# Last expert round: row-block stores on GpSimd's queue, the accumulator read in the mixing, one pair load ahead of the router

## What is computed

```python
probs = softmax(h @ router_w + router_b)
top_p, top_i = top_k(probs, 2)            # two of 8 experts for each position
gates = sum(one_hot(top_i) * top_p / sum(top_p))
for e in range(8):                        # D_FF_EXPERT = 3584
    out = out + gates[:, e] * (silu(h @ w_gate[e]) * (h @ w_up[e])) @ w_down[e]
x = x + g_f * out
return rmsnorm(x, final_norm_g)
```

## Time and profile before

| | |
|---|---|
| time, median of 3 runs | 1477.32 us (1475.62 to 1477.82) |
| the profiled execution | 1481.63 us |
| its span | 1479.8 us |
| TensorE, mean granted clock | 0.978 |
| TensorE / VectorE / ScalarE / GpSimd busy | 92% / 27% / 10% / 11% |
| moved | 499.93 MB, mean 338 GB/s |

### The profile page before, as it was taken

One profiled execution on the slowest core, in us unless ns is written; L12 is line 12 of the kernel. 1 busy time (PEld: TensorE's weight loads), 2 busy tenths in 40 slices (PEclk: granted clock), 3 DMA queues, 4 the chain that ended last, 5 costly groups with the idle time before them and its releaser, 6 DMA issues.

```text
span 1479.8 us, 43286 instructions
## 1 busy us (share of the span) xinstructions
PE 1368.2 (92%) x19076; PEld 1076.1 (73%) x19076; DVE 405.6 (27%) x1018; ACT 153.0 (10%) x364; POOL 169.3 (11%) x244
## 2 busy tenths in 40 slices
PE   4999999999998898999999999989989999998991
PEld 3887888888788786665699867767757767776770
DVE  2825251462516415111111111111111111112232
ACT  2103121000013113100000000000000000000001
POOL 0000053252203100000000000000000000000001
PEclk9999999999999999999999999999999999999995
DMA  9947577778468309489999999999999999999973
GB/s 384 423 171 310 228 273 287 271 293 303 158 225 332 125 0 401 172 343 426 426 420 417 425 410 416 426 426 410 426 425 399 427 426 407 416 424 425 415 298 127
DMA packets 52818, 499.93 MB, mean 338 GB/s; under 512 B 6668, under 2 KB 13964, under 8 KB 15372
## 3 DMA queue, kind: packets, MB, share of 16 engines
q1 hardware_dynamic: 45708, 463.36, 76.5%
q10 hardware_dynamic: 6400, 32.39, 5.8%
q0 software_dynamic: 576, 2.10, 0.4%
HBM read 485.38 MB, written 16.58 MB: 339 GB/s over the span
## 4 chain that ended last, share of the span: by engine, by line
PE 71%; DMA 17%; DVE 5%; SPq 2%; issue 2%; ACT 1%; POOL 1%; ACTq 0%; POOLq 0%; DVEq 0%
PE PS L780 29%; PE PS L484 17%; PE PS L789 14%; DMA ring<-in_expert_stream 11%; DMA arena<-in_mod_rows 4%; PE PS L634 3%; SPq L430 2%; DVE arena L1124 2%; DMA ring<-in_dense_stream 2%; PE PS L760 2%; PE PS L468 1%; PE PS L516 1%; PE PS L458 1%; DVE arena L1190 1%; PE PS L688 1%
## 5 line engine op out<-in xcount | busy, mean ns | idle before, releaser
L780 PE MATMUL PS<-ring,arena 128*32 128x256 f32 x7040 | 408.9, 380 | 24.2 <-DMA ring<-in_expert_stream 15.7
L780 PEld LDWEIGHTS PS<-ring,arena 128*32 128x32 f32 x7040 | 279.8, 110 | 127.9 <-issue 12.1
L484 PE MATMUL PS<-arena,ring 128*128 128x256 f32 x1408 | 312.8, 383 | 5.8 <-ACT arena L910 4.2
L789 PE MATMUL PS<-ring,arena 128*32 128x256 f32 x4928 | 303.1, 379 | 0.8 <-DVE consts L1124 0.8
L484 PEld LDWEIGHTS PS<-arena,ring 128*128 128x128 f32 x1408 | 269.3, 192 | 45.8 <-issue 6.7
L789 PEld LDWEIGHTS PS<-ring,arena 128*32 128x32 f32 x4928 | 198.4, 110 | 70.0 <-issue 1.8
L1124 DVE TENSOR_TENSOR stat<-stat,PS 128x128 f32<-128x128 f32 x154 | 44.4, 288 | 518.1 <-ACT stat L1073 518.1
L780 PE MATMUL PS<-arena 128*32 128x256 f32 x2816 | 164.6, 382 | 8.8 <-DMA ring<-in_expert_stream 4.6
L1732 POOL COPY arena<-arena 128x256 f32 x153 | 61.4, 402 | 796.2 <-PE PS L780 747.6
L780 PEld LDWEIGHTS PS<-arena 128*32 128x32 f32 x2816 | 115.1, 111 | 48.0 <-issue 7.3
L1124 DVE TENSOR_TENSOR arena<-arena,PS 128x256 f32 (+1 forms) x142 | 63.3, 446 | 236.1 <-PE PS L789 161.6
(11 more groups left out here) (204 smaller groups left out, 562.5 us busy)
## 6 DMA issues: line engine op xcount, KB each, us to landing
ring<-in_expert_stream SPq DMA_DIRECT2D x136, 2048.0 KB, 20.9
ring<-in_dense_stream SPq DMA_DIRECT2D x91, 1024.0 KB, 9.2
arena<-in_expert_stream SPq DMA_DIRECT2D x32, 2048.0 KB, 23.0
arena<-in_mod_rows ACTq DMA_DIRECT2D x14, 1024.0 KB, 7.2
ssm_scratch<-arena ACTq DMA_DIRECT2D x8, 1024.0 KB, 9.7
ring<-ssm_scratch SPq DMA_DIRECT2D x8, 1024.0 KB, 9.4
ring<-kc_scratch SPq DMA_DIRECT2D x32, 128.0 KB, 2.4
y_scratch<-arena SPq DMA_DIRECT2D x19, 128.0 KB
```

Source lines behind the costliest of these rows:

```text
L484: mm = pe.matmul(PS[:, bank, j * T:(j + 1) * T], w[:, c, j * P:(j + 1) * P], moving[:, c, :], start=(c == 0), stop=(c == NC - 1))
L780: mm = pe.matmul(PS[32 * q:32 * q + 32, 0, 0:256], hbuf[:, c * BLK:(c + 1) * BLK], w[:, q * 256:(q + 1) * 256], start=(c == 0), stop=(c == ...
L789: mm = pe.matmul(PS[32 * q:32 * q + 32, 1, 0:256], hidT[:, ch * BLK:(ch + 1) * BLK], w[:, q * 256:(q + 1) * 256], start=(ch == 0), stop=(c ...
```

## The change

- The four fills of `y_scr` go from ScalarE's queue to GpSimd's, behind its reversed powers and ahead of the dense FFN.
- `pair_plan` has eight slots from the start (`SOON = 1`) and the ninth from pair 24. The early one is the second half of `more`, which is made free: `places` goes to `acc`, `spread` to `reps`. Pair 7 is issued behind pair 6 once the state-space pieces are used (`AT_GLU`).
- In the last round GpSimd waits before the copy of block j (from 3 on, `BEHIND`) for `y_scaled`, and behind the copy issues the store of block j-3. All blocks but the last three are stored. `y_scaled` starts at 2, and TensorE's waits on it are shifted alike. SP only loads the gain.
- ScalarE's scalings are gone. VectorE does `keep_last` first and then, behind the last scatter, two multiply-adds for each half: first row times weight plus PSUM, second row times weight plus that. The gathers are issued half by half. The waits for the gain and for `weights_ready` are VectorE's.

```diff
 def pair_plan():
-    plan, last, queue = [], {}, list(range(RING // 2))
+    plan, last, queue = [], {}, list(range(RING // 2 + SOON))
     for n in range(PAIRS):
-        if n < RING // 2:
+        if n < RING // 2 + SOON:
             s = n
-        elif MORE_AT <= n < MORE_AT + MORE:
-            s = RING // 2 + n - MORE_AT
+        elif MORE_AT <= n < MORE_AT + MORE - SOON:
+            s = RING // 2 + SOON + n - MORE_AT
             queue.append(s)
...
+BEHIND, FILLS = 3, -(-MOST * BLK // T)
...
-        h_tm, sel, places, spread = more[:, 0:2048], more[:, 2048:3840], more[:, 3840:4736], more[:, 4736:5760]
+        h_tm, sel = more[:, 0:2048], more[:, 2048:2048 + 2 * MOST * BLK]
+        places = acc[:, 4096:4096 + MOST * BLK]
...
-        logit_t = reps[:, 256:512]
+        logit_t, spread = reps[:, 256:512], reps
...
-            s -= RING // 2
+            s = MORE - 1 - (s - RING // 2)
...
+            for n in range(RING // 2, RING // 2 + SOON):
+                sp.wait_ge(piece_done, AT_GLU)
+                load_pair(n)
             sp.wait_ge(items_ready, 1)
             upto = blocks_upto(sp)
-            for n in range(RING // 2, PAIRS):
+            for n in range(RING // 2 + SOON, PAIRS):
                 prior = PAIR_PLAN[n][1]
                 if prior is None:
                     sp.wait_ge(e_gather, GATHERS)
-                    sp.wait_ge(spread_psum, 1)
...
-            sp.wait_ge(y_filled, 16 * -(-MOST * BLK // T))
-            with sp.Fori(0, upto[LAST_E - 1] - 1) as j:
-                sp.wait_ge(y_scaled, j + 2)
-                sp.dma_start(y_scr[bass.ds(j * BLK, BLK), :].rearrange("i (q n) -> q i n", q=4),
-                             acc[:, bass.ds(j * 256, 256)]).then_inc(y_stored, 16)
             sp.wait_ge(gu_done, upto[FREE_AT] + upto[-1] * (ROUNDS - 1))
-            sp.dma_start(gain_row, ...).then_inc(y_stored, 16)
+            sp.dma_start(gain_row, ...).then_inc(gain_loaded, 16)
...
-                            pe.wait_ge(y_scaled, j)
+                            pe.wait_ge(y_scaled, j + BEHIND - 2)
...
-                if f == 4:
-                    for n in range(-(-MOST * BLK // T)):
-                        rows = min(T, MOST * BLK - n * T)
-                        act.dma_start(y_scr[n * T:n * T + rows, :], ...).then_inc(y_filled, 16)
...
-            act.wait_ge(weights_ready, 1)
-            for t_ in range(2):
-                act.wait_ge(y_back[t_], 16)
-                act.activation(y_rows[2 * t_], y_rows[2 * t_], ACT.Copy, scale=weight_of[0][:, t_:t_ + 1]).then_inc(y_part, 1)
...
-            dve.nop().then_inc(y_scaled, 1)
+            dve.nop().then_inc(y_scaled, BEHIND - 1)
...
             gate_rows(blocks - 1)
-            for t_ in range(2):
-                dve.wait_ge(y_part, t_ + 1)
-                dve.wait_ge(y_back[2 + t_], 16)
-                link(dve.scalar_tensor_tensor(y_rows[2 * t_ + 1], y_rows[2 * t_ + 1], weight_of[1][:, t_:t_ + 1], y_rows[2 * t_],
-                                              ALU.mult, ALU.add))
             dve.wait_ge(down_done, blocks * ROUNDS)
             keep_last(blocks - 1)
+            dve.wait_ge(weights_ready, 1)
             dve.wait_ge(e_scat, blocks + 2)
             for t_ in range(2):
-                tt(y_rows[2 * t_].rearrange("p (q n) -> p q n", q=4), PS[:, 4:8, t_ * T:(t_ + 1) * T],
-                   y_rows[2 * t_ + 1].rearrange("p (q n) -> p q n", q=4), ALU.add).then_inc(mixed_ready, 1)
+                y0, y1 = y_rows[2 * t_], y_rows[2 * t_ + 1]
+                dve.wait_ge(y_back[t_], 16)
+                link(dve.scalar_tensor_tensor(by_quarter(y0), by_quarter(y0), weight_of[0][:, t_:t_ + 1],
+                                              PS[:, 4:8, t_ * T:(t_ + 1) * T], ALU.mult, ALU.add))
+                dve.wait_ge(y_back[2 + t_], 16)
+                dve.scalar_tensor_tensor(y0, y1, weight_of[1][:, t_:t_ + 1], y0, ALU.mult, ALU.add).then_inc(mixed_ready, 1)
+            dve.wait_ge(gain_loaded, 16)
...
+            for n in range(FILLS):
+                rows = min(T, MOST * BLK - n * T)
+                pool.dma_start(y_scr[n * T:n * T + rows, :], ...).then_inc(y_stored, 16)
...
-            for rnd in range(1, ROUNDS):
+            for rnd in range(1, ROUNDS - 1):
...
-            pool.wait_ge(y_stored, upto[LAST_E - 1] * 16)
+            rnd = ROUNDS - 1
+            pool.wait_ge(y_stored, 16 * FILLS)
+            with pool.Fori(0, BEHIND) as j:
+                pool.wait_ge(gu_done, j + upto[-1] * rnd)
+                load_block(j).then_inc(hbuf_ready, 1)
+            with pool.Fori(BEHIND, upto[-1]) as j:
+                pool.wait_ge(gu_done, j + upto[-1] * rnd)
+                pool.wait_ge(y_scaled, j)
+                load_block(j).then_inc(hbuf_ready, 1)
+                pool.dma_start(y_scr[bass.ds(j * BLK - BEHIND * BLK, BLK), :].rearrange("i (q n) -> q i n", q=4),
+                               acc[:, bass.ds(j * 256 - BEHIND * 256, 256)]).then_inc(y_stored, 16)
+            pool.wait_ge(y_stored, upto[-1] * 16 + 16 * (FILLS - BEHIND))
...
-            for k in range(2):
-                for t_ in range(2):
+            for t_ in range(2):
+                for k in range(2):
```

More of the change, by code:

```diff
@@ L150 @@
 LAST_E = EXPERTS - 1
+BEHIND, FILLS = 3, -(-MOST * BLK // T)
+assert BEHIND <= LEAST + 1 and FILLS > BEHIND
 FREE_AT = Y_PAIR // STEP % EXPERTS
@@ L328, in trunk_kernel @@
         (down_done, acc_done, gate_part, gt_ready, gf_laid, gf_psum, gf_ready) = [sem(n) for n in "down_done acc_done gate_part gt_ready gf_laid gf_psum gf_ready".split()]
-        (y_scaled, y_stored, y_filled, y_all, y_part, slots_ready, weights_ready) = [sem(n) for n in "y_scaled y_stored y_filled y_all y_part slots_ready weights_ready".split()]
+        (y_scaled, y_stored, y_all, slots_ready, weights_ready, gain_loaded) = [sem(n) for n in "y_scaled y_stored y_all slots_ready weights_ready gain_loaded".split()]
         (mixed_ready, sum_ready, root_ready) = [sem(n) for n in "mixed_ready sum_ready root_ready".split()]
@@ L372, in blocks_upto @@
             return [eng.value_load(items[0:1, e:e + 1], min_val=LEAST * (e + 1), max_val=UPTO[e]) for e in experts]
+        AT_BT, AT_T, AT_CT = DENSE, DENSE + BATCHES, DENSE + 2 * BATCHES
+        AT_GLU = DENSE + SSM
         block = ctx.enter_context(nc.Block())
@@ L869, in _ @@
             e_down(expert_at(ROUNDS - 1, EXPERTS - 1))
-            pe.wait_ge(y_scaled, upto[-1])
+            pe.wait_ge(y_scaled, upto[-1] + BEHIND - 2)
             pe.wait_ge(gt_ready, upto[-1])
             scatter()
-            pe.wait_ge(y_scaled, upto[-1] + 1)
+            pe.wait_ge(y_scaled, upto[-1] + BEHIND - 1)
             pe.wait_ge(gt_ready, upto[-1] + 1)
@@ L1007, in _ @@
                 act.activation(f_act, PS[:, 0, :], ACT.Silu).then_inc(gate_act, 1)
-                if f == 4:
-                    for n in range(-(-MOST * BLK // T)):
-                        rows = min(T, MOST * BLK - n * T)
-                        act.dma_start(y_scr[n * T:n * T + rows, :], xt_in.rearrange("p (h d) -> (p h) d", d=D)[0:rows, :]).then_inc(y_filled, 16)
                 if f == 0:
@@ L1677, in _ @@
             s.then_inc(reversed_ready, 1)
+            for n in range(FILLS):
+                rows = min(T, MOST * BLK - n * T)
+                pool.dma_start(y_scr[n * T:n * T + rows, :], xt_in.rearrange("p (h d) -> (p h) d", d=D)[0:rows, :]).then_inc(y_stored, 16)
             pool.wait_ge(h_ready, 2 * NC)
```

8 lines of the change are left out of this document (4 added, 4 removed).

## The result

The changed kernel takes 1495.55, 1499.80 and 1502.04 us; a fourth execution, disturbed at a mean granted clock of 0.694, took 2562.91, counts in the recorded median of 1500.92 and is left out of the ratio. Before it was 1477.46: ratio 1.0146, 95% interval 1.0121 to 1.0172. It is **1.5% slower** where 1455.8 was forecast. The profiled execution took 1499.8, its span is 1498.1.

What follows compares the result with a forecast made beforehand. TensorE, busy 92% of the span, was the bound; only its idle stretches (end, expert stream, dense stage) could give time back. Terms -19.9 - 3.0 - 1.5 + 2.9 = -21.5 us gave 1455.8 us, range 1448 to 1464.

Steps and rivals of the forecast that it cites:

- GpSimd's issue: Last round, store behind each block copy: 4.8 us free per block, issue about 0.94 us, so cost 0.
- GpSimd becomes the bound: Rival, last round: store issues over 4.8 us make blocks late and the kernel slower; 1498 us at 7 us each; chance 0.04.
- X: Time to issue one GpSimd store in the last round; from 5.9 us on it eats the whole 21.5 us gain.
- The tail: End of the kernel: stores and gain row off the final path, mixing rearranged; 19.9 us gained.
- The end behind the last scatter: From the last scatter's end to the span's end: 5.3 us of mixing plus 6.5, together 11.8 us.
- The fills: Dense stage: scratch copies leave ScalarE's queue, so TensorE's stall before 328.75 goes; 1.5 us gained, bounds 0 and 4.9.
- The early pair: Expert stream: one pair loaded behind pair 6 puts the stream a pair ahead; 3.0 us gained, bounds 1.5 and 5.0.
- The stores under the stream: Last round: stores delay the pair loads and make a new TensorE stall; 2.9 us lost, bounds 0 and 5.5.
- The gathers end last: Rival, the end: store 18 lands after 12 us, the last gather is 4.7 us late; 1460.5 us; chance 0.15.
- cover of 2.8 us: The end: last gathered half there at 1449.3, wanted at 1452.1; past that, each late microsecond costs one.

Runs made afterwards that it cites:

- e1: Changed kernel with twice the room for descriptors of GpSimd's transfers (2048 bytes a partition in place of 1024): 1475.23 us, ratio 0.998.
- e10: Changed kernel without its 19 stores, so the gathers read the zeros of the fills and the output is incomplete: 1454.79 us, ratio 0.986.
- e7: e3 with the four fills of the scratch back on ScalarE in the dense stage: 1470.04 us, ratio 0.9944.
- e3: Changed kernel with only the stores put back on SyncE's queue behind its last pair: 1466.35 us, ratio 0.9936.
- e6: e3 without the early pair, its slot loaded from the gathers on as before the change: 1469.68 us, ratio 0.9936.
- e15: e14 without SyncE's wait for the last pair to land; its odd stores follow right behind that pair's issue: 1456.76 us, ratio 0.9867.
- e14: Changed kernel, GpSimd storing only even blocks with 2048 bytes of room, SyncE the odd ones after the last pair has landed: 1466.24 us, ratio 0.9929.
- e12: e3 with ScalarE storing the even blocks (10) behind its silu, SyncE the odd ones (9) behind its last pair: 1463.50 us, ratio 0.9901.

## Why the prediction was wrong

**The step that failed** is the one sentence on GpSimd's issue: "A block leaves it 5.18 - 0.40 = 4.8 us for an issue, and 0.94 is the nearest row: 0." The duration was right (0.70). What was priced was the instruction, not the state of the queue that it enters. The earlier trace rows were four gathers into idle transfer engines, 0.30 apart; they say nothing of nineteen stores into full ones. The runs showed that GpSimd stands before each issue until the store before has landed: up to 10.3 us a store and 101.0 in all, of which 29.5 fell on TensorE's path, and 11.6 more by the clock.

**The rival that came true** was named, "GpSimd becomes the bound", and its direction was right: its X, the time that a store keeps the engine, came to 101.0 / 19 + 0.7 = 6.0 on average, at which it forecast no gain. That the kernel lost more than that goes with the clock and with the unevenness of the holds (large ones cannot be paid back by small ones), which its sum did not have. But it got 0.04, because it was argued only by the duration of the issue and by VectorE's port. e1 shows the mechanism to be another: room for descriptors alone takes 25.7 of the 46.1 us that the stores cost (1500.9 to 1475.2; 1454.8 in e10), with VectorE's work unchanged.

What would have raised the chance stood in the rows: loads into the full stream took 17.9 to 22.1 us to land, and the kernel gives GpSimd's descriptors the small room of 1024 bytes. The prediction used the slow landing for the last store only. It should have asked how many stores are in flight if each takes 10 us and one comes in 5.18, and what the issuing engine does then.

**The other terms.** The tail: 19.9 forecast, 19.2 in e10; the last scatter took 2.09 us there, not the 1.15 that was put for it. The end behind the last scatter: 11.8 forecast, 11.7 in e10 (1440.33 to 1452.0). The fills: 1.5 forecast, 0.93 at the stall in e7. Their 3.67 MB, issued at 57 us, cost nothing: the window from 80 to 90 is now at a DMA share of 1.02 where it was at 0.43, and TensorE is busy throughout it in both. The early pair: 3.0 forecast; the traces of e3 and e6 give 3.2 at the last landing (1420.0 against 1423.2), of which 2.2 existed at the first issue already; the intervals of the two ratios are too wide to tell 3 from nothing, so it stays open. The stores under the stream: 2.9 forecast, 0.96 for ten of them in e15. Together, without stores, they were to give 24.4; e10 is 21.1 under before on its chip (1475.91 to 1454.79). e15 makes every store and is 21.0 under (1477.77 to 1456.76), where the forecast was 21.5 under: near for a kernel whose stores hold nobody, but in part because a gain somewhat too high and a price of the stores somewhat too high cancel. Two slips change nothing: four multiply-adds of 1.30 are 5.2, not 5.3, and the chances add up to 1.02.

**"The gathers end last"** (0.15) was right in e3 and e14 by a cause that I had not seen, the rate of 1 KB packets; in e15, where both rates are respected, its cover of 2.8 us was short by 0.8. In the changed kernel itself the mixing waited for no gather. The landing of a store under the stream had been put at 12 us by this rival; it was 10.8 for the first.

## What to carry to other kernels

A transfer's issue is cheap only while its queue drains faster than it is fed. Before putting a stream of small transfers on an engine that others wait for, multiply the landing time under load by the rate of issue: that many want to be in flight, and here the issuing engine stood in its next issue once its queue had no place for them (on GpSimd at every store, or with twice the room at every third, until all before had landed). Count packets, not bytes. If the rate is too high for one queue, split the transfers over two kinds of queue, and keep the last one on the queue that is empty.

## What the runs showed of the hardware

- GpSimd stood before every direct store with 1024 bytes of room and before every third with 2048, until all stores before it had landed, in e1 even when two of the three had landed long before.
- Why one store of 9 packets an engine takes that much room is open. The four gathers, also 144 packets each (576 in the page of before), went out 0.30 us apart in the same 1024. The four fills of the changed kernel went out unheld too, into full transfer engines: issued from 56.85 on within 2.2 us, they landed 7.3 to 14.6 us after their issue. By the count of the queue's packets (3440 less 23 times 144) they are 32 packets each, 128 in all. That fits a room counted in packets; the gathers do not.
- GpSimd's store shows 144 packets whether it carries 64 or 128 KB.
- Under a full stream of 16 KB packets a store of GpSimd's queue landed in 10 to 11 us, with three in flight the next ones 5 to 6 us behind; without the stream in 4.
- SyncE's and ScalarE's 1 KB packets ran at 98 GB/s in the windows read, at a transfer-engine share of 0.28, over one queue or two.
- TensorE's granted clock was 0.50 behind a wait of 5.23 us for the block copy, and 0.89 in the mean of a stretch with seven such waits; 1.00 in e10 without them.
- ScalarE's issue, 0.58 us else, held it for up to 16.43 us, and SyncE's for up to 15.24 in e12.
